# Conditioning weights by halves, alternating up-projections and 24 spare transposes in a hybrid RWKV / latent attention / MoE block

## The reference

```python
mod = jax.nn.silu(c) @ w_ada[l] + b_ada[l]
sh_m, sc_m, gt_m, sh_f, sc_f, gt_f = jnp.split(mod, 6, axis=-1)
h = modulate(rmsnorm(x, g_norm_mix[l]), sh_m, sc_m)      # h * (1 + scale) + shift
z = h @ w_in[l]
z_rwkv, z_mla, z_gates = jnp.split(z, [RWKV_COLS, RWKV_COLS + MLA_COLS], axis=-1)
...
w_log = -jax.nn.softplus(-(w0 + jnp.tanh(zw) @ w_decay_up)) - 0.5
a = jax.nn.sigmoid(a0 + za @ w_a_up)
```

## Time and profile before

| | |
|---|---|
| median of 3 runs | 1513.24 us (1509.96 to 1517.48) |
| profiled execution, its own time | 1519.26 us |
| its span in the profile | 1517.4 us |
| TensorE / VectorE / ScalarE / GpSimd busy | 91% / 50% / 32% / 21% of the span |
| granted TensorE clock, mean | 0.958 of full |

### The profile page before, as it was taken

How to read it: one execution, slowest core, us unless ns; L and a number is a source line. 1 busy time by engine, 2 the same in 40 slices (tenths; PEclk the granted TensorE clock), 3 DMA queues, 4 the chain that set the end, 5 groups by cost and what they waited for, 6 DMA issues and landing times. The chain is left out here.

```text
span 1517.4 us, 32870 instructions
## 1 busy us (share of the span) xinstructions
PE 1384.3 (91%) x14305; PEld 997.9 (66%) x14305; DVE 761.0 (50%) x1139; ACT 492.4 (32%) x891; POOL 313.4 (21%) x327
## 2 busy tenths in 40 slices
PE   3899999986999998799989999999996799999996
PEld 2687777735899998677767888787885333332332
DVE  3715676766677665445647555656455422111111
ACT  4433232263344443444435444413111111111110
POOL 0002221205556552011110000000000123332323
PEclk8899999997999999899999999999997699999998
DMA  9761322270000001750003113514227899999992
GB/s 373 272 187 45 91 76 63 80 269 2 4 4 4 4 11 39 208 201 15 15 15 153 56 56 110 195 46 167 84 83 275 352 345 399 382 402 376 398 364 56
DMA packets 74956, 238.20 MB, mean 157 GB/s; under 512 B 12216, under 2 KB 37304, under 8 KB 58048
## 3 DMA queue, kind: packets, MB, share of 16 engines
q1 hardware_dynamic: 63872, 219.31, 38.7%
q0 software_dynamic: 10944, 16.82, 4.6%
HBM read 207.74 MB, written 51.40 MB: 171 GB/s over the span
## 5 line engine op out<-in xcount | busy, mean ns | idle before, releaser
L3050 PE MATMUL ps<-gu,xT 128*32 128x512 f32 x1296 | 178.3, 609 | 5.0 <-DMA gu<-w_e_up 3.5
L3266 DVE TENSOR_TENSOR sg<-sg,ps 128x256 f32<-128x256 f32 x25 | 10.5, 421 | 206.6 <-ACT sg L3136 206.6
L3050 PEld LDWEIGHTS ps<-gu,xT 128*32 128x32 f32 x1296 | 46.8, 112 | 98.9 <-issue 95.3
L2937 POOL DMA_INDIRECT out<-YTM,home x48 | 75.2, 1566 | 169.3 <-DVE YTM L3275 162.0
L354 PE MATMUL ps<-hh,wr_h 128*128 128x512 f32 x224 | 94.0, 420 | 4.5 <-DVE hl L350 3.8
L355 PE MATMUL ps<-hl,wr_h 128*128 128x512 f32 x224 | 89.4, 399 | 0.0
L356 PE MATMUL ps<-hh,wr_l 128*128 128x512 f32 x224 | 89.4, 399 | 0.0
L3068 PE MATMUL ps<-dn,hidT 128*32 128x512 f32 x648 | 86.7, 592 | 0.5 <-ACT hidT L3140 0.5
L2117 DVE TENSOR_REDUCE nmax<-ps 128x1 f32<-128x896 f32 (+4 forms) x64 | 45.8, 753 | 72.3 <-PE ps L2015 71.7
L2955 POOL MEMSET xg<- 128x3072 f32 x1 | 2.7, 2657 | 366.5 <-PE ps L2442 366.5
L1285 POOL TENSOR_TENSOR off<-mats,cst 128x256 f32<-128x256 f32 x80 | 66.7, 851 | 50.9 <-PE ps L1707 50.6
(11 more groups left out here) (440 smaller groups left out, 3432.8 us busy)
## 6 DMA issues: line engine op xcount, KB each, us to landing
gu<-w_e_gate SPq DMA_DIRECT2D x29, 1024.0 KB, 17.4
gu<-w_e_up SPq DMA_DIRECT2D x29, 1024.0 KB, 23.5
dn<-w_e_down SPq DMA_DIRECT2D x29, 1024.0 KB, 18.0
wbuf<-w_ada SPq DMA_DIRECT2D x16, 1024.0 KB, 12.9
wbuf<-w_ada SPq DMA_DIRECT2D x16, 512.0 KB, 4.6
wraws<-w_gates SPq DMA_DIRECT2D x16, 512.0 KB, 4.9
wr<-w_rwkv SPq DMA_DIRECT2D x14, 512.0 KB, 3.6
qk_cols<-YTM SPq DMA_DIRECT2D x8, 768.0 KB, 5.3
```

The lines of the kernel that those rows point to most:

```text
L2937: pool.indirect_dma_start(out=out[0], out_offset=bass.IndirectOffsetOnAxis(ap=col.bitcast(u32), axis=0), in_=yo[:, buf], in_offset=None, b ...
L3050: last = nc.tensor.matmul(ps[part, GB[b]], xT[:, b, k, part], gu[expert(m, c_) % WB][:, :, k], start=(k == 0), stop=(k == KD - 1))
```

## The change

- *Constants*: only the first 128 columns (the identity) and one row of the rest are loaded early, behind two x tiles; the remainder comes behind `wm`. All eight x tiles are loaded at once, the eighth into the space of `zm`.
- *Norm of x*: roots go in four batches of two tiles; VectorE takes the squares of tiles 1 and 3; ScalarE calls a root on a dummy value first.
- *Conditioning by halves* (`HalfRows`): of each of shift and scale, first the first 512 columns (pieces k = 0 to 7, 512 KB each), then, behind the two `wr` tiles, the second 512. Half h uses bank 6 or 5 and strips at partitions 32h and 64 + 32h. The bias is now a matmul with a row of ones that opens the accumulation, and for half 0 it stands at the head of TensorE's list. ScalarE copies the shift row, VectorE makes the scale row, each half is transposed on its own (four transposes). Half 0 gives the columns of channels 0 to 3, half 1 of 4 to 7.
- *TensorE's order*: bias 0; tiles 0 to 5, products 0 and 1, tile 6, products 2 and 3, tile 7, products 4 to 7; columns 0; 24 transposes of the identity into an unused bank; channel 0; bias 1; products 0 to 3 of half 1; channel 1; products 4 to 7; channel 2; columns 1; channels 3 to 7.
- *Phase 2*: the up-projection weights are loaded in slot 8 of phase 1, `sel` at its end; the two weights alternate per half of the tokens; three semaphores become one; the store of the gate row moves to the start of phase 3.
- *Phase 3*: the memset of S and `headrk` go from VectorE to GpSimd, behind its first product.

The core of the diff:

```diff
+        class HalfRows:
+            def part(self, h, a):
+                return slice(64 * a + 32 * h, 64 * a + 32 * h + 32)
...
+            def load(self, sp, h, k):
+                src = w_ada_v[:, k, 0:2 * D].rearrange("p (a h n) -> p a h n", a=2, h=2)[:, :, h]
+                sp.dma_start(self.piece(h, k), src).then_inc(self.w_in[h][k], 16)
+
+            def biased(self, pe, h):
+                pe.wait_ge(self.b_in, 48)
+                for a in range(2):
+                    nc.tensor.matmul(ps[self.part(h, a), self.banks[h]], C("ones")[0:1, 0:32],
+                                     self.bias[0:1, a * D + h * 512:a * D + (h + 1) * 512], start=True, stop=False,
+                                     skip_group_check=True)
+
+            def products(self, pe, h, k):
+                if h == 0 and k == 0:
+                    pe.wait_ge(self.rep_s, 2)
+                pe.wait_ge(self.w_in[h][k], 16)
+                for a in range(2):
+                    m = nc.tensor.matmul(ps[self.part(h, a), self.banks[h]], self.crep[:, k], self.piece(h, k)[:, a],
+                                         start=False, stop=(k == KD - 1), skip_group_check=True)
+                m.then_inc(self.mm, 1)
...
                     sp.dma_start(ccol[:], c[0].rearrange("(p k) -> p k", k=KD)).then_inc(c_in, 16)
-                    sp.dma_start(cst[:], consts).then_inc(const_in, 16)
-                    for t in range(XT):
+                    for t in range(NT):
                         load_x(t)
+                        if t == 1:
+                            sp.dma_start(cst[:, 0:P], consts[:, 0:P]).then_inc(const_in, 16)
+                            sp.dma_start(cst[0:1, P:], consts[0:1, P:]).then_inc(const_in, 16)
                     rows0.load_bias(sp)
...
                     for k in range(KD):
-                        rows0.load(sp, k)
...
+                        rows0.load(sp, 0, k)
+                    for c_ in range(2):
+                        load_weights(c_)
+                    for k in range(KD):
+                        rows0.load(sp, 1, k)
                     sp.dma_start(wm[:], w_mla).then_inc(wm_in, 16)
...
-                            if t == NT - 1:
-                                sp.wait_ge(roped, 2 * NT)
-                                sp.dma_start(wup[0:64], w_decay_up[0]).then_inc(up_in, 16)
-                                sp.dma_start(wup[64:128], w_a_up[0]).then_inc(up_in, 16)
-                                sp.dma_start(sel[:], norm_sel).then_inc(sel_in, 16)
+                        if slot == NT:
+                            sp.dma_start(wup[0:64], w_decay_up[0]).then_inc(up_in, 16)
+                            sp.dma_start(wup[64:128], w_a_up[0]).then_inc(up_in, 16)
+                    sp.wait_ge(roped, 2 * NT)
+                    sp.dma_start(sel[:], norm_sel).then_inc(up_in, 16)
...
+                    squares(0)
+                    roots(0)
+                    squares(2)
+                    roots(1)
+                    squares(4)
+                    turned(0)
+                    squares(5)
+                    roots(2)
+                    for t in (1, 2):
+                        turned(t)
+                    for t in (6, 7):
                         squares(t)
...
+                    roots(3)
+                    for t in range(3, NT):
                         turned(t)
...
+                    rows0.shift_row(act, 0)
                     for c_ in range(2):
                         weights(c_, 16)
...
+                    pe.wait_ge(const_in, 32)
+                    rows0.biased(pe, 0)
+                    for t in range(NT):
+                        row_transposes(t)
+                        if t >= NT - 3:
+                            for k in range(2 * (t - NT + 3), 2 * (t - NT + 3) + 2 if t < NT - 1 else KD):
+                                rows0.products(pe, 0, k)
+                    row_columns(0)
+                    for i in range(WARM):
+                        nc.tensor.transpose(ps[:, 4, i % CT * P:(i % CT + 1) * P], C("ident"), C("ident"))
+                    channel(0)
+                    rows0.biased(pe, 1)
+                    for k in range(CT):
+                        rows0.products(pe, 1, k)
+                    channel(1)
+                    for k in range(CT, KD):
+                        rows0.products(pe, 1, k)
+                    channel(2)
+                    row_columns(1)
+                    for k in range(3, KD):
+                        channel(k)
...
-                    rows2.store(sp, 1)
...
+                        for n in range(2):
+                            for j, (w, src, done) in enumerate(((wup[0:64], Z(WA)[0:64], dec),
+                                                                (wup[64:128], Z(WA)[64:128], a_done))):
+                                if c_ and n == 0:
+                                    pe.wait_ge(done, c_)
                                 m = nc.tensor.matmul(ps[:, 6 * j + n], w[:, c_ * P:(c_ + 1) * P],
                                                      src[:, n * 512:(n + 1) * 512], start=True, stop=True)
-                            m.then_inc(up_mm, 1)
+                                if n:
+                                    m.then_inc(up_mm, 1)
...
+                    rows2.store(sp, 0)
...
                     prepare(0)
+                    nc.gpsimd.memset(S[:], 0.0).then_inc(init, 1)
+                    for c_ in range(CT):
+                        nc.gpsimd.tensor_scalar(headrk[:, c_], C("heads"), PC("r_k", c_), None, ALU.mult)\
+                          .then_inc(init, 1)
```

More of the change, by code:

```diff
@@ L536, in _, with roots @@
                     nc.scalar.activation(csig[:], ccol[:], ACT.Sigmoid).then_inc(c_sig, 1)
+                    act.wait_ge(const_in, 32)
+                    nc.scalar.activation(mcol[:, 0, 0, 0:1], C("ident")[:, 0:1], ACT.Sqrt)
                     def squares(t):
[L539 to L546, removed]
+                        act.wait_ge(x_in[t], 16)
+                        n = sum(i not in ON_DVE for i in range(t))
+                        if n:
+                            act.wait_ge(ssq, n)
+                        nc.scalar.activation(tmp[:], rows_of(t), ACT.Square, accum_out=ss[:, t:t + 1]).then_inc(ssq, 1)
+                    def roots(two):
+                        cols = slice(2 * two, 2 * two + 2)
+                        act.wait_ge(rstd, 2 * two + 1)
                         nc.scalar.activation(rs[:, cols], rs[:, cols], ACT.Sqrt).then_inc(root, 1)
@@ L721, in _ @@
                         low_part(hl[:, k], xn(k), hh[:, k]).then_inc(h_lo, 1)
+                    squares(1)
+                    roots(0)
+                    for t in (0, 1):
+                        scale_rows(t)
+                    squares(3)
+                    roots(1)
+                    for t in (2, 3):
+                        scale_rows(t)
+                        turned(t - 2)
+                    turned(2)
+                    roots(2)
+                    for t in (4, 5):
+                        scale_rows(t)
+                    for t in (3, 4):
+                        turned(t)
+                    roots(3)
+                    for t in (6, 7):
+                        scale_rows(t)
+                    for t in (5, 6, 7):
+                        turned(t)
+                    rows0.scale_row(dve, 0)
+                    columns(0)
+                    weights(0, 1)
+                    dve.wait_ge(mcol_s, 1)
+                    dve.wait_ge(xn_a, NT)
+                    dve.wait_ge(xn_d, NT)
+                    modulated(0)
+                    weights(1, 2)
+                    for k in range(1, CT):
+                        modulated(k)
+                    nc.vector.memset(zT[:, 0:2, 0:1], 0.0).then_inc(zero, 1)
+                    rows0.scale_row(dve, 1)
+                    columns(1)
+                    dve.wait_ge(const_in, 48)
+                    dve.wait_ge(mcol_s, 2)
+                    for k in range(CT, KD):
+                        modulated(k)
                     dve.wait_ge(wm_hi, 1)
@@ L1065, in _ @@
                     rows2.add_bias(dve, CH)
+                    dve.wait_ge(rows2.done, 1)
                 @block.tensor
@@ L1549, in _ @@
                     exponents(0)
-                    nc.vector.memset(S[:], 0.0).then_inc(init, 1)
-                    for c_ in range(CT):
-                        nc.vector.tensor_scalar(headrk[:, c_], C("heads"), PC("r_k", c_), None, ALU.mult)\
-                          .then_inc(init, 1)
                     for j in PERIODS:
```

174 lines of the change are left out of this document (82 added, 92 removed).

## The result

The changed kernel takes 1529.55 us in the median (1528.32 to 1530.57, four runs), the one before, beside it, 1515.12 (1509.96 to 1517.48, four runs): a ratio of 1.0085, interval 1.0062 to 1.0107. By that ratio it is slower by about 13 us (9 to 16; the two medians are 14.4 apart), more than the 0.5% that a measurement tells from no change. The forecast was 1511.5, in a range that ended at 1518.

A forecast was written before the change was run, and what follows sets the result against it. TensorE, busy 91% of the span, was taken as the bound, with a head that could be shortened. Head -1.85, up-projection phase -1.1 + 0.4, GpSimd move +0.8: -1.75, from 1513.24 to 1511.5 us, range 1504 to 1518.

The forecast's parts named there:

- Part 2: Channels with the second half between them: 31.5 us together, 1.0 of it waiting before channel 4; VectorE's other waits hidden.
- the forecast 73.05: Start of the latent projection in us, 74.89 before: 72.2 at full clock, plus 0.85 for the clock.
- the 1.85 us that the head was to gain: Head of the kernel: latent projection starting at 73.05 in place of 74.89.
- Part 1: Conditioning by halves: last product of half 0 over at 34.6, first channel at 40.7, 9.1 us earlier; each piece still 0.86.
- rival B: Conditioning products: two strips 64 apart do not run side by side, a piece costs 1.72; total 1527; chance 0.08.
- Rival A: Head limited by transfers, not TensorE: last product of half 0 over at 28.1, 6.5 us less, total 1505; chance 0.16.
- Part 3: 24 spare transposes before the first channel: free at full clock; clock loss there 0 to 1.7 us, taken as 0.85.
- Rival C: Spare transposes do not hold the clock: 1.7 for 0.85, 0.9 for their half-clock length, about 1 later; 1514; chance 0.14.
- Part 4: Up-projections, phase 2: earlier loads not worth 1.4, alternating 0, moved gate-row store gains 1.1, half clock costs 0.4.
- The +0.4: Phase 2 cost from a possibly longer half-clock stretch, through more idle around 314 to 320; bounds -1.6 and +1.7.
- Part 5: S and headrk to GpSimd: VectorE gain 0, GpSimd's five operations 2.5 us, net cost 0.8, slowing bounds 0 to 2.

The follow-up runs named there:

- experiment 1: Changed kernel with the constants' remainder loaded in two transfers, 112 rows from row 16 and 15 from row 1: 1518.31 us, ratio 1.0004 to the kernel before.
- experiment 2: Changed kernel, slow 127-row transfer kept, VectorE's wait for it moved behind channels 4 to 7: 1531.68 us, ratio 1.0081 to the kernel before.
- experiment 3: Kernel before with its constants loaded as row 0, then the other 127 rows: 1547.47 us, ratio 1.0193.
- experiment 4: Changed kernel with the constants' remainder as 112 rows from row 1 and 15 from row 113: 1516.39 us, ratio 1.0001 to the kernel before.
- experiment 5: Changed kernel with the constants' remainder as 122 rows from row 1 and 5 from row 123: 1515.28 us, ratio 0.9992 to the kernel before.
- experiment 9: Experiment 6 with S and headrk back on VectorE: 1509.51 us, ratio 0.9948, beside 1509.75 for the repeat of experiment 6.
- experiment 6: Experiment 1 with the bias products of half 0 moved behind tile 5: 1509.62 us, ratio 0.9947 to the kernel before; repeated, 1509.75, ratio 0.9948.
- experiment 7: Without the 24 spare transposes: on top of experiment 1, 1517.87 us, ratio 1.001; on top of experiment 6, 1510.27, ratio 0.9957.
- experiment 8: Kernel before with only the phase 2 and 3 changes: 1516.28 us, ratio 0.9989; experiment 6 without them, alternating order kept: 1512.88, ratio 0.9972.

## Why the prediction was wrong

**The step that failed** is one clause of Part 2: that VectorE's other waits, "the constants' remainder, landing near 43", are hidden, and "if they were not, each would be worth under 1". The wait was seen; its transfer was priced at the stream's 420 GB/s of the earlier trace rows, as if it were like every other, and none of the rows of before shows a transfer with a row count like 127. The constants went in one piece of 128 rows then. The bound below 1 us had nothing under it: a transfer of a shape that no row shows should have been bounded by what one engine of 16 moves, by the earlier trace rows 420 / 16 = 26 GB/s, which makes 24 us of 626 KB (an estimate from these rows). It landed at 69.2 in place of 43, the gap ahead of channel 4 was 6.62 us in place of 1.0, and experiments 1 to 5 show cause and size.

**From the forecast 73.05 to 84.10** there are 11.0 us, by the steps of the sum:

- First TensorE work at 16.36, not 14.9 (1.5): the wait for bias and gains was the right releaser, but they landed 1.5 later. Up to the first channel 0.7 more is lost, so 42.84 for 40.7.
- Gap before channel 4, 6.62, not 1.0 (5.6): the failed step.
- Half clock behind that gap (1.4): channel 4 to the latent projection takes 12.72, in experiment 1 11.27. It belongs to the failed step too.
- Half clock in the first channel: after had the whole price, some 1.6 as in experiment 9 (34.1 against 32.5), not the 0.85 taken (0.8 more).
- The channels at full clock take 32.5, not 31.5 (1.0). By the distances of starts in experiment 6, bias and four products take 4.53 (37.41 to 41.94) for 4.30, and the other four 3.56 (44.93 to 48.49) for 3.44: 0.35 of it. The 0.86 of a product was a little low already: four of before take 3.57, from 35.54 to 39.11. The rest of this 1.0 has no place.

The terms make 11.0. Without the fault the latent projection starts at 74.8 to 75.3 (experiments 1, 4, 5) where 73.05 was expected, and the totals, 1.0004, 1.0001 and 0.9992 of before, can't be told from the forecast's 0.9988. That agreement tells little: the 1.85 us that the head was to gain did not come (its latent projection starts within 0.5 of before's 74.89, on either side), and what the rear parts gave is of the size of the scatter.

**Part 1.** That a piece in two strips costs no more than one in four was right (0.9), and rival B (two strips 64 apart do not overlap) falls: four matmuls would have taken 1.7. Rival A had the right time at the wrong place: it put the last product of half 0 over at 28.1. In the change it was over at 36.9, since the bias wait holds every transpose; with that wait behind tile 5 it is over at 28.5.

**Part 3.** The clock's price was left between its ends; no single trace lies there: of the nine with the spare transposes six have none of it and three the whole. In experiment 6 TensorE did nothing but transposes from 9.30, and they are 206 ns apart up to 12.6 (16 in 3.30 us) and 118 behind it (18 in 2.13 busy us).

```profile
9.30:12.60 3.30, 3.30 (x16) 3.30 (x17) 2.89 (x7) 1.38 (x5) 0.00 (x0) 1.00 1.02 417
12.70:16.20 3.50, 2.13 (x18) 1.65 (x16) 3.19 (x8) 2.51 (x7) 0.00 (x0) 1.00 1.04 325
```

The view prints 1.00 for both stretches, as it did for the half-clock rate at 14.46 in the earlier trace rows, so the rate is what tells: the clock rose after transposes alone. The Trainium skill, "TensorE: Matmul & The Clock Gate", Part 4: PE-mode transpose, says that they do not count as busy for it in the same way; these fp32 ones raised it. Rival C (they never hold the clock) falls with that and with experiment 7, although in after itself the clock did fall in the first channel. C also priced the transposes at half clock at 0.9 of delay, where the prediction's own 5.1 us in a space of 4.8 give 0.3; in the nine traces they ran at full clock.

**Part 4.** The trace of after, for the earlier trace rows:

```profile
323.11 1.99 PE L1188 MATMUL ps<-zT,YTM 64*128 64x512 f32 x8 [1.65 <-DMA norm_sel<-norm_sel]
...
332.18 1.94 PE L332 MATMUL ps<-wbuf,crep 128*32 128x512 f32 x8
334.05 3.65 PE L1188 MATMUL ps<-zT,YTM 64*128 64x512 f32 x8
...
353.48 1.12 SPq L345 DMA_DIRECT2D mod_rows<-YTM  x4
353.81 2.24 DVE L1563 TENSOR_TENSOR_SCAN cum<-cst,lw 128x128 f32<-128x128 f32 x4 [0.82 <-DVEq L1116]
```

Up-projections that alternate take 1.99 for eight, 2.00 before: 0, as forecast. They still wait for a load (`sel`, issued at the end of phase 1): TensorE starts 1.18 us behind ScalarE's first square, 1.48 before, so little of the earlier start came. VectorE's idle time at the boundary is 0.82 for 1.69: 0.9 of the 1.1 forecast. In after it was eaten by the clock: product and up-projections take 1.94 and 3.65, at half clock to their end, for 1.79 and 2.92 in the earlier trace rows. The +0.4 taken for that stands beside the list of traces with the rear parts in experiment 8, against the 3.4 us of half clock that before had: 1.5 more in five traces, none in six, 0.7 in the mean.

**Part 5.** GpSimd took more than the 2.5 taken:

```profile
354.72 0.53 POOL L1403 MEMSET S<- 128x512 f32 x1
355.23 3.25 POOL L1405 TENSOR_SCALAR zT<-cst,pc 128x128 f32<-128x128 f32 x4
358.68 1.77 POOL L1365 TENSOR_TENSOR ce<-aa,ex 128x512 f32<-128x512 f32 x1 [0.20 <-ACT ex L1436]
```

3.8 us, yet it is free 0.2 before ScalarE's exponential lets it go on, which GpSimd waited 3.72 for in the version with these on VectorE. The cover was there; the cost is some 0.16 (experiment 9), not 0.8.

## What to carry to other kernels

When a change cuts a transfer, look at the number of rows of each piece before its bytes: a table of 128 rows that leaves out one of them for an earlier load is 127 rows, and it moved at 26 GB/s where the stream of the earlier trace rows had 350 to 419. Moving the wait of a slow transfer did not help here, since other transfers that TensorE needs are issued behind it; ask of each wait at the head of an engine's list what stands behind it that needs none of it, for here that was worth 8 us, all that the repaired change gains over the kernel before.

## What the runs showed of the hardware

- Engines by row count: 127 rows a DMA share of 0.06 and 26 GB/s, 122 rows 0.12 and 52 GB/s, 112 rows full share; from row 1 or row 16 alike.
- SP's issue of DMAs is held up behind such a transfer: 21.8 us for four small ones (2.8 otherwise), 27.0 for seven x tiles (3.7 in the kernel before). With two engines none of TensorE's work was held up, though issuing the five rows behind them took 6.8 us in place of 0.5 to 0.6.
- One and the same kernel (experiment 6 and its repeat) has 6.8 us at half clock in phase 2 in one execution and 3.4 in the other, 31.9 and 30.3 us from first square to first scan; in the first channel kernels with the same code there have none or 3.4. Each 3.4 is worth 1.4 to 1.7 us, as much as several terms of the sum.
- TensorE's clock rises under fp32 transposes alone: in experiment 6 they go from 206 ns apart to 118 with nothing else on the engine.
